# Dilated attention: even and odd heads' logits issued alternately into two banks, with one mask matmul for a whole bank ahead of them

## What is computed

```python
# forgetting attention: 16 heads of 64, two query blocks of 128
logits = einsum(q[:, :, qs:qe], k[:, :, :qe]) + cum_q - cum_k
p = softmax(where(causal, logits, -inf)); out = einsum(p, v[:, :, :qe])
# dilated attention: 8 heads of 64, rotary on q and k
DILATED_PAIRS = ((128, 1), (512, 4), (2048, 16))
for window, dilation in DILATED_PAIRS:
    o, lse = dilated_window_attention(qh, kh, vh, window, dilation)
weights = softmax(stack(lses)); y = sum(weights * stack(outs))
```

## Time and profile before

| | us |
|---|---|
| median of 3 runs | 757.69 (756.62 to 758.19) |
| the profiled execution | 756.58 |
| its span in the trace | 754.8 |
| TensorE busy / VectorE busy / ScalarE busy | 723.3 / 508.5 / 379.2 |
| mean granted clock of TensorE | 0.982 of full |

### The profile page before, as it was taken

The page is one execution under the profiler, slowest core; times in us unless marked ns, Lnnn a source line. Parts: engine busy times, 40 slices in busy tenths (PEclk is TensorE's granted clock), DMA queues, the critical chain, the costliest instruction groups (busy, mean ns, idle before and its releaser), DMA issues.

```text
span 754.8 us, 9396 instructions
## 1 busy us (share of the span) xinstructions
PE 723.3 (96%) x3550; PEld 593.2 (79%) x3550; DVE 508.5 (67%) x727; ACT 379.2 (50%) x559; POOL 22.7 (3%) x36
## 2 busy tenths in 40 slices
PE   5899999999999999999999999999999999999996
PEld 4687777778877778878887788877887888888885
DVE  4787998796855758745668779945675555555445
ACT  5337443454534656554545764534556544444343
POOL 4100000000000000000002100000000000000000
PEclk8799999999999999999999999989999999999999
DMA  9997765667674456832355553413365565655521
GB/s 299 370 319 271 272 222 191 223 214 241 226 262 120 145 197 220 268 117 85 111 168 153 160 163 113 137 59 95 125 199 187 180 189 179 189 190 179 195 74 56
DMA packets 74476, 138.95 MB, mean 184 GB/s; under 512 B 5748, under 2 KB 18272, under 8 KB 74432
## 3 DMA queue, kind: packets, MB, share of 16 engines
q1 hardware_dynamic: 72816, 134.82, 54.7%
q0 software_dynamic: 880, 1.64, 0.7%
q10 hardware_dynamic: 736, 1.90, 0.7%
HBM read 137.30 MB, written 1.05 MB: 183 GB/s over the span
## 4 chain that ended last, share of the span: by engine, by line
PE 85%; DVE 9%; issue 2%; ACT 2%; DMA 1%; SPq 0%; DVEq 0%; ACTq 0%
PE G L348 22%; PE G L350 21%; PE G L349 21%; PE T L369 4%; PE T L667 3%; DVE arena L970 2%; DVE wlo L970 2%; PE T L696 2%; PE T L793 2%; PE G L433 1%; DMA arena<-in_mod_w_dram 1%; DVE arena L979 1%; PE G L434 1%; PE G L435 1%; PE T L590 1%
## 5 line engine op out<-in xcount | busy, mean ns | idle before, releaser
L970 DVE TENSOR_TENSOR wlo<-raw,whi 128x1024 fp32r<-128x1024 f32 x206 | 251.1, 1222 | 137.4 <-ACT whi L1718 136.5
L348 PE MATMUL G<-whi,ahi 128*128 128x512 f32 x776 | 315.4, 406 | 6.0 <-DVE wlo L970 5.5
L350 PE MATMUL G<-whi,alo 128*128 128x512 f32 x776 | 305.0, 393 | 0.0
L349 PE MATMUL G<-wlo,ahi 128*128 128x512 f32 x776 | 304.5, 392 | 0.0
L1718 ACT ACTIVATE whi<-raw 128x1024 fp32r<-128x1024 f32 x206 | 217.2, 1058 | 133.7 <-PE G L350 120.6
L348 PEld LDWEIGHTS G<-whi,ahi 128*128 128x128 f32 x776 | 147.0, 189 | 38.7 <-DVE wlo L970 8.6
L350 PEld LDWEIGHTS G<-whi,alo 128*128 128x128 f32 x776 | 146.7, 189 | 31.9
L349 PEld LDWEIGHTS G<-wlo,ahi 128*128 128x128 f32 x776 | 147.1, 190 | 29.3 <-issue 1.4
L1720 ACT ACTIVATE arena<-T,st 128x128 f32<-128x128 f32 (+1 forms) x48 | 16.9, 419 | 49.0 <-DVE st L1347 49.0
L1720 ACT ACT_TABLE_LOAD x27 | 34.6, 1283 | 2.2 <-issue 1.8
L1718 ACT ACTIVATE ahi<-T 128x512 fp32r<-128x512 f32 x25 | 15.0, 599 | 40.6 <-PE T L369 40.6
(11 more groups left out here) (209 smaller groups left out, 632.2 us busy)
## 6 DMA issues: line engine op xcount, KB each, us to landing
raw<-in_ret_w_in_dram SPq DMA_DIRECT2D x48, 512.0 KB, 5.4
raw<-in_w_gate_up_dram SPq DMA_DIRECT2D x40, 512.0 KB, 3.7
raw<-in_mod_w_dram SPq DMA_DIRECT2D x32, 512.0 KB, 5.2
raw<-in_fox_w_in_dram SPq DMA_DIRECT2D x32, 512.0 KB, 4.7
raw<-in_w_in_dram SPq DMA_DIRECT2D x28, 512.0 KB, 3.6
raw<-in_w_down_dram SPq DMA_DIRECT2D x22, 512.0 KB, 4.3
arena<-in_mod_w_dram SPq DMA_DIRECT2D x16, 512.0 KB, 8.3
raw<-in_ret_w_out_dram SPq DMA_DIRECT2D x16, 512.0 KB, 5.5
```

Of the source, the lines that this page charges most:

```text
L348: e.matmul(o, ah, wh, start=first and k == 0, stop=False)
L349: e.matmul(o, ah, wl, start=False, stop=False)
L350: done = e.matmul(o, al, wh, start=False, stop=last and k == 1)
L970: e.tensor_tensor(o, a, b, op).then_inc(sig[name], 1)
```

## The change

1. `mdb` now holds the mask of the older block first and the causal one second, so that the two together are one row of 256 as a bank with m = 1 wants it.
2. A mask becomes one bf16 matmul of 512 columns for a whole bank, ahead of the logits, which then accumulate on it: in FOX for its 4 groups with m = 0 (before: 4 matmuls of 128 columns in each), in WIN for all 6 groups. FOX's 8 groups with m = 1 keep their one mask of 128 columns for every head.
3. WIN's groups are made anew: (0, 2, 4, 6) and (1, 3, 5, 7) with m = 0, then (0, 2), (1, 3), (4, 6), (5, 7) with m = 1. Each holds heads of one half of the partitions.
4. WIN's logits are issued for two groups at a time, at the place of the even-numbered group: two banks are taken, both masks issued, then the heads of the even bank and of the odd bank by turns. There is no `win_swap`.
5. Every WIN group has its own bank for the values and its own division: 6 reciprocals and 6 multiplications in place of 4 and 4.
6. `left_mix(0)` needs the values of group 3 and stands one unit later, ahead of V4.

```diff
-C_ID, C_TRI, C_INV, C_MD, C_MO, C_CT, C_CS, C_DEC = 0, 128, 256, 384, 512, 640, 1024, 1152
+C_ID, C_TRI, C_INV, C_MO, C_MD, C_CT, C_CS, C_DEC = 0, 128, 256, 384, 512, 640, 1024, 1152
...
+def win_groups():
+
+    return [(0, (0, 2, 4, 6)), (0, (1, 3, 5, 7)), (1, (0, 2)), (1, (1, 3)), (1, (4, 6)), (1, (5, 7))]
...
+            def diagonal(t):
+
+                e.matmul(t[:, :].rearrange("p (h n) -> p h n", h=4), idb[:, :], mdb[:, 1:2, :].to_broadcast([P, 4, P]), start=True, stop=False)
...
+                if m == 0:
+                    diagonal(t)
+                for a, h in enumerate(hs):
+                    o = t[:, a * nk:(a + 1) * nk]
+                    d = e.matmul(o, qF[0:66, h, m * P:(m + 1) * P], kF[0:66, h, 0:nk], start=m > 0, stop=m == 0 and a == 3)
+                    if m:
+                        d = e.matmul(o[:, P:nk], idb[:, :], mdb[:, 1, :], start=False, stop=True)
...
+            def win_logits(g):
+
+                if g % 2:
+                    return
+                m, heads = WIN[g][0], (WIN[g][1], WIN[g + 1][1])
+                nk = P * (m + 1)
+                on_.wait_ge(sig["wqk"], 4)
+                on_.wait_ge(sig["masks"], 2)
+                t = [bank(("win", "logits", g + z), sig["win_exp"], g + z + 1) for z in range(2)]
+                for z in range(2):
+                    if m == 0:
+                        diagonal(t[z])
+                    else:
+                        e.matmul(t[z][:, :].rearrange("p (h a n) -> p h a n", h=2, a=2), idb[:, :],
+                                 mdb[:, None, :, :].to_broadcast([P, 2, 2, P]), start=True, stop=False)
+                for a in range(len(heads[0])):
+                    for z in range(2):
+                        h, half = heads[z][a], slice(64 * z, 64 * z + 64)
+                        d = e.matmul(t[z][:, a * nk:(a + 1) * nk], qA[half, h // 2, m * P:(m + 1) * P], kA[half, h // 2, 0:nk], start=False,
+                                     stop=a + 1 == len(heads[0]))
...
+            def win_values(g):
+                m, heads = WIN[g]
+                on_.wait_ge(sig["win_turned"], g + 1)
+                on_.wait_ge(sig["vaw"], 2)
+                t = bank(("win", "values", g), sig["win_out"], 2 * g + 2)
...
-                if k == 1:
-                    left_mix(0, ("win_out", 4))
+                if k == 2:
+                    left_mix(0, ("win_out", 8))
```

More of the change, by code:

```diff
@@ L301, in program @@
         bank_of = {}
-        FOX = attention_groups((0, 4, 8, 12))
-        WIN = attention_groups((0, 4))
+        FOX = fox_groups()
+        WIN = win_groups()
         def raw_tile(n):
@@ L647, in _ @@
                     freed(b, m, "aug", 3 * (2 * c + m) + 1)
[L650 to L702, removed]
@@ new lines, in _, with fox_values @@
+            fox_held = {}
+            def fox_values(g):
+                h0, m, hs = FOX[g]
+                first, last = g == 0 or FOX[g - 1][:2] != (h0, m), g + 1 == len(FOX) or FOX[g + 1][:2] != (h0, m)
+                o = 2 * (h0 // 4) + m
+                on_.wait_ge(sig["fox_turned"], g + 1)
+                on_.wait_ge(sig["va"], 2 * (h0 // 8) + 2)
+                if first:
+                    fox_held["o"] = bank(("fox", "values", o), sig["fox_out"], 2 * o + 2, hold=True)
+                t = fox_held["o"]
+                for a, h in enumerate(hs):
+                    c0 = 65 * (h - h0)
+                    for j in range(m + 1):
+                        d = e.matmul(t[:, c0:c0 + 65], PTf[:, g % 2, (a * (m + 1) + j) * P:(a * (m + 1) + j + 1) * P],
+                                     va[:, j, h, :], start=j == 0, stop=j == m)
+                d.then_inc(sig["fox_values"], 1)
+                if last:
+                    held.discard(bank_of["fox", "values", o])
@@ new lines, in win_values @@
+            def win_values(g):
[3 more added lines that the diff above has]
+                t = bank(("win", "values", g), sig["win_out"], 2 * g + 2)
+                for a, h in enumerate(heads):
+                    for j in range(m + 1):
+                        d = e.matmul(t[:, 65 * a:65 * a + 65], PTw[:, g % 2, (a * (m + 1) + j) * P:(a * (m + 1) + j + 1) * P],
+                                     vaw[:, j, h, :], start=j == 0, stop=j == m)
+                d.then_inc(sig["win_values"], 1)
@@ L704, in _ @@
             steps = attention_steps(len(FOX))
-            fox = attention("fox", FOX, lambda h, m: qF[0:66, h, m * P:(m + 1) * P], lambda h, n: kF[0:66, h, 0:n], va,
-                            False, False, lambda h0: [("va", 2 * (h0 // 8) + 2)],
-                            lambda h0: [("heads", 8 + 4 * (h0 // 8) + 2 + h0 // 4 % 2 + 1)])
+            fox = {"logits": fox_logits, "flip": lambda g: flip("fox", g, PBf), "values": fox_values}
             def left_of(k, c):
@@ L855, in _ @@
             steps = attention_steps(len(WIN))
-            win = attention("win", WIN, lambda h, m: qA[64 * (h % 2):64 * (h % 2) + 64, h // 2, m * P:(m + 1) * P],
-                            lambda h, n: kA[64 * (h % 2):64 * (h % 2) + 64, h // 2, 0:n], vaw,
-                            True, True, lambda h0: [("vaw", 2)], lambda h0: [("wqk", 4)])
+            win = {"logits": win_logits, "flip": lambda g: flip("win", g, PBw), "values": win_values}
             def left_mix(k, *done):
@@ L905, in _ @@
                 if n == 0:
-                    left_mix(2, ("win_out", 8))
+                    left_mix(2, ("win_out", 12))
                 elif n >= 2:
@@ L1349, in flip @@
                 def flip(g):
-                    m = groups[g][1]
+                    m = groups[g][-2]
                     t, o = T[bank_of[name, "flip", g]], PT[:, g % 2, :]
```

44 lines of the change are left out of this document (34 added, 10 removed).

## The result

| | before | after |
|---|---|---|
| median, us | 757.15 (4 runs, 756.57 to 758.19) | 745.62 (4 runs, 745.11 to 746.02) |
| span of the profiled execution | 754.8 | 743.8 |
| its mean granted clock | 0.982 | 0.986 |

The ratio is 0.9853, with a 95% interval of 0.9827 to 0.9879: faster by 11.5 us, where 8.6 was forecast. A later comparison with more runs gives 745.94 (5 runs) against 756.61 (20 runs), 0.9874 (0.9842 to 0.9906).

A forecast was written before the change was run, and what follows sets the result against it. TensorE, busy 96% of the span, was taken as the bound. WIN 5.1, FOX 0.5 and the clock 3.0 sum to 8.6 us off 756.6: 748.0, plus 1.1 gives 749.1 us; range 746.5 to 753.5.

The forecast's parts named there:

- (a): Possible wait at group 0's flip, one unit (2.8 us) behind the first pair; 2.0 us needed, 0.8 us of room.
- (b): Possible wait of group 1's values for group 3's exponential, because of bank T0; 0.9 us of room, group 3's values similarly.
- The price of a round trip: WIN's TensorE going into 64 partitions and back: 0.20 plus 0.10 us, for 16 heads-by-block 4.8 us in all.
- loads keep their pace: Assumption for WIN's logits: weight loads leave 128-column records no overlap, so first pair 2.54 us, others 1.84, 5.1 saved.
- 9 and 5 slots: WIN's upper bound: halves side by side need 9 and 5 slots, not 16 and 8; 5.9 us saved.
- full overlap: Rival: WIN's two halves run fully side by side and the dip goes; 9.4 us saved, 748.3 us; 15%.
- FOX: One mask per m = 0 group drops three of four steps back to float32; 0.5 us over four groups, bounds 0 and 1.0.
- The clock: The clock's dip in WIN's group 1 and the unit behind it goes with shorter stretches; 3.0 us saved, bounds 0 and 3.0.
- Carrying this over: The median's 1.1 us above the profiled execution is added to 748.0, giving 749.1 us.
- Slower: Rival: each of 13 changes of half in WIN costs 0.30 us, 3.9 in all, and the clock falls more; 763 us; 2%.
- Logits in a row: Rival: WIN's logits pass one after another and the dip goes; 7.3 us saved, 750.4 us; 25%.
- The dip stays: Rival: the clock's dip in WIN stays or moves; only 5.6 us saved, 752.1 us (751.3 to 753.4); 15%.

The follow-up runs named there:

- fox_only: The kernel before with only FOX's mask changed: one mask of 512 columns ahead of the four heads in groups with m = 0; 753.2 us, ratio 0.9966.

## Why the prediction was wrong

- **What bounds it: right.** TensorE's busy time and the span fell by the same 11.0 us, and no wait took anything back. The waits (a) and (b), the room of `left_mix(0)` and VectorE's added work cost nothing, as worked out.
- **The price of a round trip, 0.30: right.** Five more of them cost 1.44, 0.29 each. It missed only 0.09 ahead of each entry, in the instruction before: 0.45 us over five entries. The 0.10 that it booked as "coming out" is this same price. The last mask of group 4, with a flip behind it, passes in 0.06 us, as two rows of the kernel before show; in the earlier trace rows the mask with a logit behind it takes 0.15.

```profile
516.35 0.22 PE L670 MATMUL T<-mdb,idb 128*128 128x128 bf16 x1
516.41 0.61 PE L369 MATMUL T<-head,arena 128*128 128x128 f32 x4
```

- **The failed step: "loads keep their pace".** I held that with records of 128 columns loads leave nothing to overlap, "so the first pair stays at 2.54 and the others come to 1.84". The loads of the two halves overlap as the matmuls do: two begin at once. The pairs took 1.62, 1.59 and 1.59 where 2.54, 1.84 and 1.84 were forecast, so the saving within WIN's groups was 6.5 us, not 5.1. Even the upper bound of 5.9 was too low, since it gave the second half a slot of its own ("9 and 5 slots"): the rows fit 8 and 4, that is 0.111 and twice 0.215 less. The duration of a load that I used, 187 to 193 ns, came from 128 loads into the whole array; it says how long a load takes and nothing of two halves. "Bound by loads" should have been one end and "free second half" the other, and the choice between them left open. The nearest rival was full overlap, at 748.3. The rule of the Trainium skill ("TensorE: Matmul & The Clock Gate", Part 3) that loads and matmuls of different row groups run together is what this case's rows show: 16 records in 1.09 us, 8 of one half in 1.09. The second half of the rule that the prediction names from the Trainium skill ("TensorEngine Tiling (Array Packing)", Key Properties), that going from tile to tile within a mode drains nothing, agrees with 0.060 us per alternating record.
- **FOX: right, slightly low.** 0.67 against 0.5. Three steps of 0.06 back to float32 in each of four groups, 0.7 us, go almost wholly.
- **The clock: right in size, wrong in its reason.** 3.0 forecast, 2.83 by moving a group alone, 2.95 left in the ledger, 3.15 by the rows of the kernel before. But the argument, that a stretch of 4.6 us brings it down and group 3's 2.35 does not, falls: stretches of 4.5 and 7.2 us kept it at 1.00, and a fall behind group 3 was traced. So this term came out right by luck as much as by reason; what makes the clock fall stays open. The Trainium skill ("TensorE: Matmul & The Clock Gate", HAM oscillation) ties a fall to gaps in which TensorE waits; here TensorE is busy 2.00 of 2.00 us from 494 to 498 and its longest gap ahead is the 0.20 of the earlier trace rows, so the rule does not explain this one.
- **"Carrying this over", 1.1 us: wrong.** The median of before lay 1.1 above its profiled execution because its runs spread with the clock, and not for a reason that the changed kernel shares. The changed kernel's median equals its profiled execution, 745.6. This 1.1, with the 1.4 of the pairs, the 0.45 of the entries, the 0.17 of FOX and the 0.44 of the start's scatter, less the 0.05 by which the clock gave less than its 3.0, makes the 3.5 us between forecast and result.
- **The rivals.** Slower: refuted, a change of half costs nothing. Logits in a row: they overlap even when issued in a row, which none of the prediction's cases had. The dip stays: it went, in every trace of the changed kernel.

## What to carry to other kernels

Where matmuls use only half of the partitions, give each bank the heads of one half, take two banks, and put the two halves close to each other in the list: the second half then cost nothing here (16 records in 1.09 us, 8 of one half in 1.09). Group what works in another tiling mode (masks by an identity matmul above all) into as few runs as possible, ahead of or behind the whole bank, at the 0.3 us that a round trip cost here. When a kernel's runs lie in bunches, look at the mean granted clock of each before a difference between medians is put down to an edit.

## What the runs showed of the hardware that was not expected

- Half-array float32 records cost 0.060 us each when the halves alternate and 0.116 when they don't (128 columns, 48 records). Each record has its weight load, so the loads of the two halves overlap as well.
- The two halves overlap also when they are issued one after the other, from a few records away: four records of the other half ahead cost nothing, eight cost 0.55 us.
- One bf16 matmul of 512 columns whose second operand is one block of 128 columns repeated four times passes at the same 0.23 us as a unit's: FOX's first in the changed kernel stands at 324.29 and the logits behind it at 324.52.
- The clock can fall to the 1.2 GHz level with TensorE busy throughout. It falls also behind short waits, and not in every execution of a program: ahead of the recurrence's stage TensorE idles twice, 0.69 to 0.70 and 1.24 us, in both profiled executions of the changed kernel; the clock fell in the first and not in the second, as the two rows below show. That is 106.43 against 104.87 us for the distance between FOX and the recurrence, 1.6 us between two executions of one program. Over all the traces it is not even: the six with the old WIN all have this fall, of the twelve with the new WIN only the first. WIN comes later, and FOX's masks do not decide it (`fox_only` has the fall), so what does stays open; a difference of this size between two medians may hang on it.

The changed kernel, first profile:

```profile
416.00:418.00 2.00, 2.00 (x7) 1.51 (x6) 2.00 (x5) 1.91 (x7) 1.30 (x2) 0.50 0.31 62
```

The changed kernel, profiled again:

```profile
416.00:418.00 2.00, 2.00 (x11) 1.65 (x10) 2.00 (x3) 1.75 (x6) 1.78 (x2) 1.00 0.31 29
```
